# Building the expert-side one-hots on ScalarE and moving 22 gathered rows ahead of the last phase

## The reference, cut to what matters

```
def block(xt):                       # 128 tokens
    q = (xt @ wq).reshape(128, 8, 2, 128)
    s1, s2 = scores of q[:, :, 0] and q[:, :, 1] against 128 keys each
    v1, i1 = lax.top_k(s1, 16);  v2, i2 = lax.top_k(s2, 16)
    sc, ci = lax.top_k(all 256 sums of v1 and v2, 16)
    e = i1[ci // 16] * 128 + i2[ci % 16]        # expert's number
    g = softmax(sc)
    act = gelu(einsum('thkd,td->thk', u[e], xt))
    return einsum('thk,thkd->td', g * act, v[e])
```

## Time and profile before

| | us |
|---|---|
| median of 3 runs | 1545.89 (1543.62 to 1549.62) |
| profiled execution | 1550.2 |
| its span, first to last instruction | 1548.4 |
| PE busy in the span | 1421.3 (92%) |
| DVE busy | 1138.4 (74%) |
| ACT busy | 293.5 (19%) |
| POOL busy | 656.1 (42%) |

### The profile page before, as it was taken

One profiled execution on the slowest core, in us unless ns is written; L12 is line 12 of the kernel. 1 busy time (PEld: TensorE's weight loads), 2 busy tenths in 40 slices (PEclk: granted clock), 3 DMA queues, 4 the chain that ended last, 5 costly groups with the idle time before them and its releaser, 6 DMA issues.

```text
span 1548.4 us, 20472 instructions
## 1 busy us (share of the span) xinstructions
PE 1421.3 (92%) x7586; PEld 1278.6 (83%) x7586; DVE 1138.4 (74%) x2391; ACT 293.5 (19%) x833; POOL 656.1 (42%) x580
## 2 busy tenths in 40 slices
PE   7899998879999899899999999999999999999403
PEld 7798787765557666899999999999999999999402
DVE  1412799987787879999989999997444465556787
ACT  2611213621010111111124444341000000000000
POOL 0000445465575362222225566565333344444771
PEclk9999998879999999999999999999999999999756
DMA  8486888777999796888889999999999999999993
GB/s 328 166 287 227 326 283 310 274 241 270 396 393 391 278 414 235 281 295 287 274 298 343 382 369 378 376 371 399 409 396 391 409 409 408 409 408 409 359 371 144
DMA packets 136340, 518.42 MB, mean 335 GB/s; under 512 B 15793, under 2 KB 18609, under 8 KB 127793
## 3 DMA queue, kind: packets, MB, share of 16 engines
q0 software_dynamic: 82944, 302.03, 51.9%
q1 hardware_dynamic: 53296, 215.09, 36.9%
HBM read 513.88 MB, written 3.15 MB: 334 GB/s over the span
## 4 chain that ended last, share of the span: by engine, by line
PE 43%; DMA 22%; DVE 17%; issue 9%; POOL 6%; ACT 2%; SPq 0%; DVEq 0%; POOLq 0%
DMA arena<-v_d,arena 17%; PE bank L858 13%; PE bank L746 7%; PE bank L588 4%; POOL arena L1754 3%; DVE arena L1255 3%; PE bank L876 3%; PE bank L562 3%; DMA arena<-u_d,arena 3%; DVE arena L1516 3%; POOL arena L1744 3%; DVE arena L1512 2%; PE bank L838 2%; PE bank L758 2%; PE bank L760 2%
## 5 line engine op out<-in xcount | busy, mean ns | idle before, releaser
L1744 POOL DMA_INDIRECT arena<-u_d,arena x256 | 324.4, 1267 | 401.6 <-DVE arena L1244 175.3
L1744 POOL DMA_INDIRECT arena<-v_d,arena x256 | 258.6, 1010 | 425.0 <-DVE arena L1255 359.1
L1255 DVE SCALAR_TENSOR_TENSOR arena<-arena 128x1024 f32<-128x1024 f32 x254 | 316.9, 1281 | 158.2 <-DMA arena<-v_d,arena 155.4
L858 PE MATMUL bank<-arena 128*128 128x224 f32 x2048 | 399.6, 354 | 4.8 <-DMA arena<-u_cols_d 4.8
L882 PEld LDWEIGHTS bank<-arena 128*128 128x128 f32 x2112 | 391.5, 191 | 1.4 <-issue 1.4
L882 PE MATMUL bank<-arena 128*128 128x224 f32 (+2 forms) x2112 | 391.9, 349 | 0.0
L858 PEld LDWEIGHTS bank<-arena 128*128 128x128 f32 x2048 | 385.1, 191 | 5.5 <-issue 5.0
L1244 DVE CUSTOM_DVE_ANT_0 arena<-arena 128x1024 f32<-128x1024 f32 x288 | 341.7, 1220 | 62.9 <-DMA arena<-u_d,arena 51.6
L838 PE MATMUL bank<-arena 128*128 128x128 f32 (+1 forms) x512 | 115.5, 385 | 1.4 <-ACT arena L1081 1.4
L746 PE MATMUL bank<-arena 128*128 128x128 f32 (+1 forms) x512 | 113.7, 383 | 0.1
L838 PEld LDWEIGHTS bank<-arena 128*128 128x128 f32 x512 | 78.2, 193 | 35.0 <-ACT arena L1081 2.1
(11 more groups left out here) (229 smaller groups left out, 1220.9 us busy)
## 6 DMA issues: line engine op xcount, KB each, us to landing
arena<-w_items_d SPq DMA_DIRECT2D x66, 1024.0 KB, 6.5
arena<-u_cols_d SPq DMA_DIRECT2D x128, 512.0 KB, 5.6
arena<-v_cols_d SPq DMA_DIRECT2D x128, 512.0 KB, 7.9
arena<-u_d,arena POOLq DMA_INDIRECT x256, 6.9
arena<-v_d,arena POOLq DMA_INDIRECT x256, 8.5
arena<-ln_d SPq DMA_DIRECT2D x4, 512.0 KB, 10.2
out_d<-arena SPq DMA_DIRECT2D x8, 256.0 KB, 4.2
arena<-xT_d SPq DMA_DIRECT2D x1, 1536.0 KB, 18.4
```

What stands on the lines that cost most here:

```text
L858: last = mm(bank[:, 4 + c % 2, 0:ND], u_buf[:, c % UBUFS, k, :], B.act_in[:, k, P:P + ND], start=k == 0, stop=k == KC - 1)
L1255: v.scalar_tensor_tensor(out=to, in0=rows[:, s, :], scalar=wv[:, k:k + 1], in1=to, op0=ALU.mult, op1=ALU.add).then_inc(row_used, 1)
L1744: pool.indirect_dma_start(rows[:, r % SLOTS, :], None, table, bass.IndirectOffsetOnAxis(eidx[:, t, k:k + 1], 0)).then_inc(landed[r % SLOTS ...
```

## The change

Three things are done together. First, for every quad (`by_scalar` is true for all) DVE's `one_hot` compares the first half only, and ScalarE builds the second half with its gates from the iota: four instructions form |index - iota| (Abs, with the index as bias and a scale of -1), a wait on these, and four form Relu(gate - gate x |index - iota|), which is the gate where the index matches and zero elsewhere. For that `copy_picks` makes one more copy, of the negated gates (`ngT`). TensorE's `spread` waits for DVE's half and ScalarE's half separately. Second, `copy_gates` goes through its elements in another order: it reads PSUM with a step and writes runs of four in a row, where it read in a row and wrote with a step. Third, the stages move: the exponentials, the transposes and the spread come five blocks later, the spread ends four blocks later, and the counts of rows become 8, 8 and 134 where they were 6, 7 and 124.

```diff
-EXP_AT = 53
-TURN_AT = 55
-SPREAD_AT, SPREAD_END = 56, 122
-EXTRA_AT = 64
+EXP_AT = 58
+TURN_AT = 60
+SPREAD_AT, SPREAD_END = 61, 126
+EXTRA_AT = 69
...
-EARLY_ROWS, PAIR_ROWS, HALF_ROWS = 192, 6, 7
-HOT_ROWS = 124
-MID_ROWS = 368
+EARLY_ROWS, PAIR_ROWS, HALF_ROWS = 192, 8, 8
+HOT_ROWS = 134
...
+def by_scalar(q):
+
+    return q >= 0
+
+
+def apart_by(q):
+
+    return sum(by_scalar(k) for k in range(q + 1))
...
+        ngT = [gate_w[:, 0, :, :].rearrange("p h k -> p (h k)"), view(194, NE)]
...
             def spread(q):
 
+                pe.wait_ge(hot_raw, q + 1)
                 pe.wait_ge(hot_ready, q + 1)
...
                 fn(idxT[d], bank[:, 6 + d, 0:2 * P].rearrange("p (k t) -> p k t", k=2), ACT.Copy).then_inc(pick_out, 1)
+                fn(ngT[d], bank[:, 6 + d, 2 * P:3 * P], ACT.Copy, scale=-1.0).then_inc(pick_out, 1)
                 fn(gT[d], bank[:, 6 + d, 2 * P:3 * P], ACT.Copy).then_inc(pick_out, 1)
 
             def copy_gates(q, c):
 
                 act.wait_ge(g_done, q + 1)
-                fn(w_high[:, c + 1 - LOW:, q * QUAD:(q + 1) * QUAD].rearrange("p e t -> p t e"),
-                   bank[:, 6 + q % 2, :].rearrange("p (t e) -> p t e", t=QUAD)[:, :, c + 1:], ACT.Copy).then_inc(g_out, 1)
+                fn(w_high[:, c + 1 - LOW:, q * QUAD:(q + 1) * QUAD],
+                   bank[:, 6 + q % 2, :].rearrange("p (t e) -> p e t", t=QUAD)[:, c + 1:, :], ACT.Copy).then_inc(g_out, 1)
 
             def scale_hot(q):
 
+                d, t = divmod(q * QUAD, P)
+                if by_scalar(q):
+                    if t == 0:
+                        act.wait_ge(pick_out, 3 * (d + 1))
+                    if q >= 2:
+                        act.wait_ge(g_done, q - 1)
+                    for j in range(QUAD):
+                        last = fn(hot[:, q % 2, QUAD + j, :], iota[:, :], ACT.Abs, scale=-1.0,
+                                  bias=idxT[d][:, 1, t + j:t + j + 1])
+                    last.then_inc(hot_apart, 1)
+                    act.wait_ge(hot_apart, apart_by(q))
+                    for j in range(QUAD):
+                        one = hot[:, q % 2, QUAD + j, :]
+                        last = fn(one, one, ACT.Relu, scale=ngT[d][:, t + j:t + j + 1], bias=gT[d][:, t + j:t + j + 1])
+                    last.then_inc(hot_ready, 1)
+                    return
                 act.wait_ge(hot_raw, q + 1)
-                d, t = divmod(q * QUAD, P)
...
-                both = [P, 2, QUAD, NK]
-                v.tensor_tensor(hot[:, q % 2, :, :].rearrange("p (k j) e -> p k j e", k=2),
+                halves = 1 if by_scalar(q) else 2
+                both = [P, halves, QUAD, NK]
+                v.tensor_tensor(hot[:, q % 2, 0:halves * QUAD, :].rearrange("p (k j) e -> p k j e", k=halves),
                                 iota[:, :].unsqueeze(1).unsqueeze(1).to_broadcast(both),
-                                idxT[d][:, :, t:t + QUAD].unsqueeze(3).to_broadcast(both), ALU.is_equal).then_inc(hot_raw, 1)
+                                idxT[d][:, 0:halves, t:t + QUAD].unsqueeze(3).to_broadcast(both), ALU.is_equal).then_inc(hot_raw, 1)
```

More of the change, by code:

```diff
@@ L318, in build @@
         hot_raw = sem("hot_raw")
+        hot_apart = sem("hot_apart")
         hot_ready = sem("hot_ready")
@@ L941, in _ @@
                 if c == SPREAD_AT:
-                    pe.wait_ge(pick_out, 2 * len(DENSE))
+                    pe.wait_ge(pick_out, 3 * len(DENSE))
                 hidden(c)
@@ L1613, in one_hot @@
                 if t == 0:
-                    dve.wait_ge(pick_out, 2 * (d + 1))
+                    dve.wait_ge(pick_out, 3 * (d + 1))
                 if q >= 2:
                     dve.wait_ge(g_done, q - 1)
-                both = [P, 2, QUAD, NK]
-                v.tensor_tensor(hot[:, q % 2, :, :].rearrange("p (k j) e -> p k j e", k=2),
+                halves = 1 if by_scalar(q) else 2
+                both = [P, halves, QUAD, NK]
+                v.tensor_tensor(hot[:, q % 2, 0:halves * QUAD, :].rearrange("p (k j) e -> p k j e", k=halves),
                                 iota[:, :].unsqueeze(1).unsqueeze(1).to_broadcast(both),
-                                idxT[d][:, :, t:t + QUAD].unsqueeze(3).to_broadcast(both), ALU.is_equal).then_inc(hot_raw, 1)
+                                idxT[d][:, 0:halves, t:t + QUAD].unsqueeze(3).to_broadcast(both), ALU.is_equal).then_inc(hot_raw, 1)
             def take_gates(q, c):
```

## The result

| | median of the runs, us | lowest to highest | ratio to before (95%) |
|---|---|---|---|
| before, same session | 1547.76 | 1543.62 to 1551.84 | |
| changed | 1524.79 | 1521.31 to 1525.51 | 0.9845 (0.9823 to 0.9868) |

The change takes 23.0 us off the median. The profiled execution of the changed kernel took 1521.31 us, with a span of 1519.5. Its lines are shifted: L869 is the hidden blocks, L888 the spread, L894 the sums, L878 the turned picks, L1149 the gate copy, L1161 and L1167 the Abs and the Relu, L1647 DVE's one-hots, L1658 and L1659 its taking of the gates, L1272 a u row, L1283 a v row, L1330 the sum of the rows, L935 the fold.

A forecast was written before the change was run, and what follows sets the result against it. It took DVE's list of gathered rows, at a used-up transfer rate in the last phase, to set the end. Terms: -32.4 + 6.4 + 1 = -25.0 us, giving 1525 profiled, 1521 from the median; range 1509 to 1542.

The forecast's parts named there:

- Rows moved: End of DVE's row list: 22 rows fall out at 1.47 us each, a gross gain of 32.4 us.
- a sign against itself: Last phase: the prediction counts as wrong if the extra rows go slower than 1.47 us each.
- Routing, 12 more rows: Routing stage: DVE ends 14.3 us later, TensorE arrives 15.2 later; cost 0, or 0.7 us of wait.
- One-hots on ScalarE: Spread stage: ScalarE's added Abs and Relu end near +3.5 of 3.92 us per quad; cost 0, upper end 30 us.
- +3.92 for every quad: Spread stage: TensorE takes up the next quad 3.92 us after a hidden block's end (0.89 spread, 3.03 hidden block).
- the rival's boundary: Spread stage, table-loads rival (chance 0.08, 1625 us): a loss begins where a quad takes ScalarE over 4.8 us.
- Waits: Spread stage: DVE's taking of gates waits for a gate copy some 1.6 us later; TensorE does not notice.
- Bandwidth in the spread stage: Spread stage: 134 rows ask for 410 GB/s; at 400 reached, 257 us become 263, costing 6.4 us.
- the range given: End of the spread stage: the first sum was to come between 1072 and 1082 us.
- Start of the sums: Start of last phase: first v load near 1065.5, not 1060.23, about 5 us late; +1 us at the end, 0 to 3.
- What makes the gain: Spread stage: ScalarE's one-hots free 30 us of DVE time, 10 more rows take 12, so DVE keeps up.

The follow-up runs named there:

- onehots_without_rows: One-hots and gate copy as changed, but stages and row counts as in the kernel before: 1554.87 us, ratio 1.0029 to before.
- rows_without_onehots: Changed kernel with one-hots built as before (DVE compares both halves, ScalarE multiplies), rows as changed: 1523.84 us, ratio 0.9838 to before.
- the pair of six-row kernels: Changed kernel with six more rows at DVE's wait for the first quad: 1517.71 us with ScalarE's one-hots, 1523.44 with one-hots as before the change.
- gate_copy_first: Changed kernel with the gate copy ahead of the one-hots in each step, these scaled one step further ahead: 1521.23 us, ratio 0.9812 to before.
- six_rows_without_onehots: Changed kernel with six more rows at DVE's wait for the first quad, one-hots built as before the change: 1523.44 us, ratio 0.9828 to before.
- old_gate_copy: Changed kernel with the gate copy in its old order (read in a row, written with a step): 1524.23 us, ratio 0.9830 to before.

## Why the prediction was right, and which of its steps were not

The forecast was 25.0 us less, and from the median 1521. Measured were 23.0 less in medians, 25.3 along the way counted from the first hidden block. The total holds; its terms don't all, and that it holds so closely is in part luck.

- **Rows moved** (32.4 us from 22 x 1.47). The last phase got 35.0 shorter, 1.59 us a row: right in size, but the picture was wrong. The extra rows got slower, which the prediction had named as a sign against itself. The first now starts at 1385.35 and not at 1431.55, so that 64 rows take 110.8 us, 1.73 each, as half of them fall in the time of the v stream:

```profile
1385.35 1.23 DVE L1272 CUSTOM_DVE_ANT_0 arena<-arena 128x1024 f32<-128x1024 f32 x1
...
1496.13 1.22 DVE L1330 TENSOR_TENSOR arena<-arena 128x1024 f32<-128x1024 f32 x1
```

  The 22 rows fell out ahead of them, where 144 rows took 360.0 us before (1071.6 to 1431.55) and 122 take 308.5 now, 2.5 each: -51.5 there and +16.6 for the extra rows make -35. Transfers price it better than DVE's list does: 22 x 0.524 MB at 407 GB/s is 28.3 us, and the tail's idle time falls by 6.5.
- **Routing, 12 more rows** (cost 0, with up to 0.7 of wait). The price of the rows held. I take a stretch of DVE's routing that begins and ends with the same two instructions in both kernels: a top-8 search (starts at 577.72 before, 576.01 after) and the subtraction that gives the arguments of the gates' exponentials (797.48 before, 809.14 after). It is 219.8 us long before and 233.1 after: 13.4 more, for 14.3 forecast, and TensorE comes 15.2 later. Yet TensorE waits 3.4 us for the picks. It was early, since its hidden loop began 52.9 us after that top-8 search before and only 50.2 us after it in the changed kernel:

```profile
630.58 9.74 PE L858 MATMUL bank<-arena 128*128 128x224 f32 x37 [4.84 <-DMA arena<-u_cols_d]
...
626.21 14.05 PE L869 MATMUL bank<-arena 128*128 128x224 f32 x73 [1.66 <-DMA arena<-u_cols_d]
```

  In the profile of before TensorE had waited 4.84 us for its first u block, and then ran with a granted clock of 0.50 (1.2 GHz) up to 634; in the changed one it had waited 1.66 us, and the clock was 1.00. And onehots_gate_copy_first, which has none of the 12 rows, began 49.3 us after its top-8 search and waited 5.7 us. So the wait is no measure of the rows' price, but goes with the start of the loop, which differs between executions for a reason that no run shows. Behind it the clock adds some. Windows around the wait:

```profile
808.00:811.00 3.00, 0.05 (x1) 0.00 (x0) 2.69 (x7) 1.52 (x2) 2.58 (x2) 1.00 0.60 202
811.00:814.00 3.00, 2.55 (x11) 2.17 (x12) 2.36 (x5) 2.02 (x9) 0.16 (x1) 0.72 0.88 285
814.00:818.00 4.00, 4.00 (x18) 3.82 (x17) 3.15 (x7) 0.36 (x1) 1.68 (x1) 0.78 0.13 54
```

  After 3 us without a matmul the granted clock is 0.72 and 0.78 for 7 us, a mix of 1.2 and 2.4 GHz, and the 48 matmuls behind the picks take 10.91 us where they took 9.25 in rows_without_onehots: 1.7 more. In the other kernels with these 12 rows the wait was between 0.4 and 3.6 us, in onehots_without_rows none. The term should have had that spread.
- **One-hots on ScalarE** (cost 0). Each price held: Relu 483 ns, Abs 396, Relus ready at +3.46, which leaves 0.46 us. What failed is "+3.92 for every quad": after a step without a quad it is 3.03, and ScalarE's list can't run ahead through such a step. With the same blind spot the rival's boundary (a loss from 4.8 us of ScalarE per quad, because steps without a quad give time back) was too high. At 4.49 the kernel is already 0.4% slower than before; taken as linear from the changed kernel with its 3.92, the gain is gone at about 4.4.

```profile
L1167 ACT ACTIVATE arena<-arena,chunk_mask 128x128 f32<-128x128 f32 x128 | 52.8, 483 | 1.1
...
L1161 ACT ACTIVATE arena<-iota,chunk_mask 128x128 f32<-128x128 f32 x128 | 40.6, 396 | 0.0
```

  These are the groups by form of the spread stage. The Trainium skill (ScalarE: Activation LUTs, Table sets: the hidden batching unit) has abs and relu in every set; the trace now agrees, as no load stands between them and the Gelus. The Trainium skill's rule that relu belongs on VectorE (ScalarE: Activation LUTs, Rules for kernel authors) fits onehots_without_rows (1.0029) and does not fit the pair of six-row kernels, where the freed VectorE time is worth some 6 us (1517.71 against 1523.44).
- **Waits** (TensorE unaffected by the later gate copy). The gate copy ends at +3.72 in the step above and not at +2.33, 1.4 us later for 1.6 forecast. DVE waits for it (1.05 us in that step, 25.3 over 38 times), and TensorE's list names no wait for the release of that bank: its waits at quads are those for one-hots.
- **Bandwidth in the spread stage** (+6.4 for 400 GB/s). The stage runs at 403, and u rows land in 7.8 us, not 11. DVE does not wait for them in the changed kernel, but its waits for gate copies hide how near the limit was: without those (gate_copy_first) it waits 15.0 us for u rows at the same 134 rows and 408 GB/s, and with 144 rows 20.7 us. So the rate was used up, as forecast. What failed is its price: TensorE hardly paid for it, as the way to the first sum is 442.4 us in gate_copy_first and 441.0 before. The first sum of the changed kernel came at 1076.9, inside the range given, for another reason: waits for picks and one-hots, the slowed blocks and the first v block. These were put at nothing (the first v block at 1), and took the place of this term at about its size (9.7 against 7.4 with the start of the sums). That is luck, the more so as the wait for the picks goes with the start of the loop in that execution.
- **Start of the sums** (+1 at the end). The first v load goes out at 1069.47, 9.2 us later than before, and TensorE waits 1.4 us for it where the prediction had about 5. What that costs at the end no run shows by itself.
- **What makes the gain.** The prediction had ScalarE's one-hots give DVE the room for the rows. That step is refuted at 22 rows (rows_without_onehots), and at 28 the runs speak for it (six_rows_without_onehots).

Open: whether the late gate copy and the late Relus cost the changed kernel anything at its end (0 to 5 us by gate_copy_first), since the wait for the picks differs by as much from one profiled kernel to the next. Not run: the later stages without the 12 rows in routing, so that those two are known only together; and six rows spread over the steps. Not tried: filling the 40 us of idle transfer time up to 800 us, where DVE is full with routing.

## What to carry to other kernels

Where the same bytes move whatever the order, multiply each stretch's length by its rate, look for the stretches below the best rate, and move transfers there: six rows in such a stretch gained 0.4 to 0.6%, ten in full ones nothing. A helper engine that issues in order cannot use steps in which its own work is light if its list first waits for the paced engine; count the room from the tightest step, not from the usual one. A change in two halves deserves a run of each half, and of each half with a little more load: what looks idle at one size can be what the next size needs.

## What the runs showed of the hardware

- A ScalarE copy that steps through its PSUM input and writes SBUF in runs of four took 0.36 us for 256 elements. The order of before, which reads in a row and steps at every element of its output, took 0.59 us for the same 256 in old_gate_copy (0.65 for 276). I had estimated 0.55 for the new order.
- At the same rate u rows landed in 7.8 us in the spread stage and v rows in 14.5 in the last phase, so in this kernel a landing time alone does not say how full the transfers are:

```profile
arena<-u_d,arena POOLq DMA_INDIRECT x120, 7.8
...
arena<-v_d,arena POOLq DMA_INDIRECT x120, 14.5
```
